# Inverse of the RWKV solve from its transposed twin: 32x32 block transposes on the vector engine in place of a third family of products

## What is computed

```python
def step(state, inp):
    r_t, w_t, k_t, v_t, a_t, b_t = inp
    sa = jnp.einsum("bhvk,bhk->bhv", state, a_t)
    state = (state * w_t[:, :, None, :] + sa[..., None] * b_t[:, :, None, :]
             + v_t[..., None] * k_t[:, :, None, :])
    return state, jnp.einsum("bhvk,bhk->bhv", state, r_t)
...
merged = (jax.nn.sigmoid(z[..., 0:D]) * (ya @ w_merge_a[l])
          + jax.nn.sigmoid(z[..., D:2 * D]) * (yb @ w_merge_b[l])
          + jax.nn.sigmoid(z[..., 2 * D:3 * D]) * (yc @ w_merge_c[l]))
```

## Time and profile before

| | |
|---|---|
| median of 3 runs | 1112.46 us (1112.19, 1112.46, 1114.2) |
| profiled execution, span from first to last instruction | 1114.1 us |
| PE busy | 1096.3 us, 98% |
| DVE busy | 839.7 us, 75% |
| ACT busy | 582.3 us, 52% |
| L2078, products of the solve, both layers | 1792 records, 58.3 us of matmul |

### The profile page before, as it was taken

One profiled execution on the slowest core, in us unless ns is written; L12 is line 12 of the kernel. 1 busy time (PEld: TensorE's weight loads), 2 busy tenths in 40 slices (PEclk: granted clock), 3 DMA queues, 4 the chain that ended last, 5 costly groups with the idle time before them and its releaser, 6 DMA issues.

```text
span 1114.1 us, 24347 instructions
## 1 busy us (share of the span) xinstructions
PE 1096.3 (98%) x10172; PEld 1006.3 (90%) x10172; DVE 839.7 (75%) x1245; ACT 582.3 (52%) x894; POOL 125.6 (11%) x142
## 2 busy tenths in 40 slices
PE   8999999999999999999999999999999999999997
PEld 7889987888789999999989999888887999999997
DVE  4798998665478798987758899957545878888763
ACT  2266577622275666663455575772226556666533
POOL 0100000146002000001110000003530010000001
PEclk8999999999999999999999999999999999999999
DMA  9946555444145566668845546351513465555551
GB/s 379 340 161 224 175 193 210 153 153 154 60 168 227 189 241 230 230 241 288 313 153 190 189 158 231 151 208 59 212 56 151 161 256 189 188 185 183 216 209 38
DMA packets 41464, 214.88 MB, mean 193 GB/s; under 512 B 7936, under 2 KB 8320, under 8 KB 22048
## 3 DMA queue, kind: packets, MB, share of 16 engines
q1 hardware_dynamic: 29856, 171.65, 41.9%
q0 software_dynamic: 11520, 41.95, 10.5%
HBM read 212.01 MB, written 1.05 MB: 191 GB/s over the span
## 4 chain that ended last, share of the span: by engine, by line
PE 95%; DVE 2%; ACT 2%; issue 1%; DMA 0%; DVEq 0%; ACTq 0%
PE ps L1780 17%; PE ps L1778 17%; PE ps L1779 17%; PE ps L1967 6%; PE ps L1969 6%; PE ps L1973 6%; PE ps L1798 5%; PE ps L2078 5%; PE ps L1737 1%; PE ps L2252 1%; PE ps L1755 1%; PE ps L2069 1%; PE ps L2056 1%; PE ps L1994 1%; PE ps L1924 1%
## 5 line engine op out<-in xcount | busy, mean ns | idle before, releaser
L963 ACT ACTIVATE WH<-ring 128x1024 fp32r<-128x1024 f32 x144 | 151.9, 1060 | 164.6 <-PE ps L1780 157.4
L1628 DVE TENSOR_TENSOR WLO<-ring,WH 128x1024 fp32r<-128x1024 f32 x144 | 175.7, 1233 | 70.0 <-ACT WH L963 70.0
L1780 PE MATMUL ps<-HH,WLO 128*128 128x256 f32 x736 | 208.1, 283 | 0.0
L1779 PE MATMUL ps<-HL,WH 128*128 128x256 f32 x736 | 206.6, 281 | 0.0
L1778 PE MATMUL ps<-HH,WH 128*128 128x256 f32 x736 | 205.0, 279 | 0.0
L1780 PEld LDWEIGHTS ps<-HH,WLO 128*128 128x128 f32 x736 | 138.7, 188 | 0.0
L1778 PEld LDWEIGHTS ps<-HH,WH 128*128 128x128 f32 x736 | 138.5, 188 | 0.0
L1779 PEld LDWEIGHTS ps<-HL,WH 128*128 128x128 f32 x736 | 138.0, 188 | 0.0
L561 POOL DMA_DIRECT2D mring<-wmod_dram x80 | 43.2, 540 | 759.4 <-DVE macc L1113 447.6
L1780 PE MATMUL ps<-GH,WLO 128*128 128x256 f32 x384 | 108.3, 282 | 0.0
L1778 PE MATMUL ps<-GH,WH 128*128 128x256 f32 x384 | 108.2, 282 | 0.0
(11 more groups left out here) (403 smaller groups left out, 2592.7 us busy)
## 6 DMA issues: line engine op xcount, KB each, us to landing
ring<-wmain_dram SPq DMA_DIRECT2D x150, 1024.0 KB, 4.9
mring<-wmod_dram POOLq DMA_DIRECT2D x80, 512.0 KB, 5.0
G<-wmod_dram SPq DMA_DIRECT2D x3, 1024.0 KB, 9.7
R<-wmod_dram SPq DMA_DIRECT2D x3, 1024.0 KB, 17.5
TK<-wmod_dram SPq DMA_DIRECT2D x2, 1024.0 KB, 20.7
X<-x_t_dram SPq DMA_DIRECT2D x1, 1024.0 KB, 5.2
y_dram<-H SPq DMA_DIRECT2D x4, 256.0 KB, 2.2
SW<-small_dram SPq DMA_DIRECT2D x1, 512.0 KB, 13.8
```

The costliest lines, as they stand in the source:

```text
L963: A(WH[:, n % 2, part], ring[:, b, part], ACT.Copy).then_inc(hi_ready, 1)
L1628: V.tensor_tensor(WLO[:, n % 2, part], ring[:, b, part], WH[:, n % 2, part].bitcast(F32), ALU.subtract).then_inc(lo_ready, 1)
L1779: MM(out, w_high[:, at], low, start=False, stop=False, skip_group_check=True)
L1780: return MM(out, w_low[:, at], high, start=False, stop=stop, skip_group_check=True)
```

## The change

Step `xt` is gone. After the additions to `TTm` of both parities in a level v < 4, DVE transposes each 32x32 block of `TTm` into `Tm` (`V.transpose`, 128x512, one for a parity). Up to that level T has nothing outside diagonal blocks of 32, so the blocks' transposes are the whole transpose. Step `x` of the next level waits for this on a new semaphore. The fill table has two entries for a level in place of three, and DVE's work between the steps stands at other points.

```diff
-FILL = [8, 32, 48, 32, 36, 8, 20, 8] + [8] + [6, 8, 6] * 4 + [6, 6, 0]
+FILL = [8, 32, 48, 32, 36, 8, 20, 8] + [8] + [8, 8] * 4 + [6, 0]
...
-        for kind in ("m", "x", "xt"):
-            if kind == "xt" and v == len(LEVELS) - 1:
-                continue
+        for kind in ("m", "x"):
...
                         if par == 1 and v == 0:
                             branch_low(1, YBL[:, :, :], YB[:, :, :], YH[:, :, :])
-                        elif par == 1 and v != 2:
-                            dve_chunks((0, 20, 0, 23, 25)[v], (0, 21, 0, 24, 26)[v])
+                        elif par == 1:
+                            mod_beside(1)
                     else:
-                        T_ = (TTm if kind == "x" else Tm)[:, par]
-                        V.tensor_tensor(T_, T_, oct(b), ALU.add).then_inc(t_ev, 1)
-                        if par == 1 and v < 4:
-                            if (kind, v) in (("x", 0), ("xt", 1), ("x", 2), ("xt", 3)):
-                                dve_chunks((19, 21, 22, 24)[v], (20, 22, 23, 25)[v])
+                        V.tensor_tensor(TTm[:, par], TTm[:, par], oct(b), ALU.add).then_inc(t_ev, 1)
+                        if par == 1 and v < len(LEVELS) - 1:
+                            for p2 in range(2):
+                                dve.wait_ge(t_ev, base + step_no("x", p2, v) + 1)
+                                V.transpose(flat(Tm[:, p2]), flat(TTm[:, p2])).then_inc(t_turned, 1)
+                            if v == 3:
+                                gated(2)
                             mod_beside(1)
...
-                    elif kind == "x":
+                    else:
                         pe.wait_ge(t_ev, base + step_no("m", par, v) + 1)
                         if v:
-                            pe.wait_ge(t_ev, base + step_no("xt", par, v - 1) + 1)
+                            pe.wait_ge(t_turned, 8 * l + 2 * (v - 1) + par + 1)
                         block_products(b, Tm[:, par], Mm[:, par], t_mm)
-                    else:
-                        block_products(b, Mm[:, par], Tm[:, par], t_mm)
                     if par == 1:
-                        fill(LEVEL0 + 3 * v + ("m", "x", "xt").index(kind))
+                        fill(LEVEL0 + 2 * v + ("m", "x").index(kind))
```

More of the change, by code:

```diff
@@ L432, in trunk_kernel @@
                                             sem("akv_summed"), sem("akv_ready"))
+        t_turned = sem("solve_turned")
         zy_mm, zy_ev, rb_mm, rb_ev = sem("zy_summed"), sem("zy_ready"), sem("read_products"), sem("read_ready")
```

## The result

| | before | after |
|---|---|---|
| median | 1112.53 us (4 runs, 1112.19 to 1114.2) | 1136.86 us (4 runs, 1127.47 to 1146.91) |
| ratio of after to before | | 1.0181, 95% interval 1.0144 to 1.0218 |
| span of the profiled execution | 1114.1 us | 1134.4 us |
| mean granted clock over it | 0.990 | 0.966 |

The kernel got slower by about 1.8%. The forecast was 1103.4 us, its range ended at 1107.8, and 0.94 of the chance lay on faster. The scatter is new as well: the four executions of after lie 19 us apart, those of before 2 us.

What follows compares the result with a forecast made beforehand. PE, busy for 98% of the span, was taken as the bound. -17.7 (steps) + 1.8 + 5.8 (waits) - 1.4 (`YCL`) + 2.4 (clock) = -9.1 us, from 1112.46 to 1103.4 us; range 1099.8 to 1107.8.

Steps and rivals of the forecast that it cites:

- What goes: PE in the solve: eight `xt` steps of 2.21 us vanish, 17.7 us saved; stream products are only moved.
- What DVE does instead: DVE in the solve: each 128x512 transpose takes 0.65 us, near an addition's 0.69; upper bound 1.34 us.
- The estimate of 1.24 us: DVE transpose priced from the skill page, four 128x128 two-byte tiles at 311 ns; sum worse by 1.5 us.
- rivals that rest on slow transposes: Solve on DVE: transposes of 1.1 to 1.34 us, 1105.5 to 1107.5 us, chance 0.17; about 2.4 us, 1118 us, 0.04.
- Is it hidden?: Solve levels: PE covers DVE's transposes, up to 1.7 us at levels 0 to 2, 0.87 us at level 3.
- I add nothing: Solve levels: the tightest modulation transfer lands half a microsecond late, using only DVE idle time; no cost.
- First new wait: PE at L2120, behind the last `x`: waits 0.9 us for the last addition, 1.8 us over two layers.
- Second new wait: PE before the read part: late `gated(3)` delays the masks, 2.9 us a time, 5.8 us in all.
- What comes back: PE before merge 4: the wait for `YCL` goes, 1.4 us gained over two layers.
- The clock: Behind the read-part wait, both layers: half speed for some 3.3 us, 1.2 us a layer, 2.4 us in all.
- the clock holds: Rival: the clock stays up through the 2.9 us wait before the read part; -11.5 us, 1101.0 us, chance 0.27.
- The slower one: Rival in the solve: transposes of say 2.4 us delay masks and `x` steps; +5.7 us, 1118 us, chance 0.04.

Runs made afterwards that it cites:

- both: Kernel after with six products behind the last `x`, FILL_ZY 10 for 6, and level 4's modulation step moved behind the last additions: 1096.89 us, 0.9853.
- behind: Kernel before, all products kept and no transposes, only the fills of the solve cut by 22 products: 1137.05 us, 1.0256.
- mod_moved: Kernel after with the modulation step behind level 4's masks moved behind the last additions, ahead of `gated(3)`: 1127.84 us, 1.014.
- zy16: Kernel after with FILL_ZY 16 for 6, so merge 3 ends before the read products: 1104.33 us, 0.9925.
- chain8: Kernel after with eight stream products in place of four at each gap of the chain: 1123.29 us, 1.0115.
- spread: Fastest repaired kernel (1096.89 us) with modulation steps in pairs behind the transposes and `gated(2)` behind level 4's masks: 1100.13 us, 0.9891.

## Why the prediction was wrong

- **What goes** was right: 1280 records for 1792, and both's account closes to 2.7 us with 17.7.
- **What DVE does instead** was right: 0.68 us for 0.65, between the bounds. The estimate of 1.24 us was almost twice too long. The rivals that rest on slow transposes are out.
- **Is it hidden?** held at the levels: L2079 waits 1.5 us in all, and transfers that landed late (DVE idle for 1.1 us before 246.56, for 0.16 us before 258.34) used up idle time only. But the count took 1.2 us for every modulation step, and three in each layer took 2.8 to 3.3 us. "I add nothing" should have been 1.5 us.
- **First new wait** failed in its size: "L2120 will wait for 0.9 us" took 2.85. The step "the last addition ends 2.85 us after the `x` starts" took DVE as free then. `behind` and mod_moved, where it is free, gave 0.8. Worth 2 x 1.95 = 3.9 us.
- **Second new wait** was right to a tenth: 2.85 us for 2.9.
- **What comes back** was right: the `YCL` wait is gone.
- **The clock** is the step that failed, in the price and not in the place: "I expect the fall behind the second new wait, in both layers" came true, but priced from the earlier trace rows at "some 3.3 us" of half clock, 1.2 us a layer. It measured 15.9 and 9.3 us. In those rows the fall had 128x512 products of the stream and full 128x128 transposes behind it; here it has the chain, groups of small products with four products of the stream between them, and the clock did not come back for 20 to 37 us. I took the length of a fall as fixed where it depends on what PE does afterwards. A fall behind the first new wait, 1.6 us in layer 0, was not in the sum at all. The runs zy16, behind and chain8 together show this: wait away, no long fall; wait without transposes, the long fall; denser chain, a shorter one.
- **The rivals.** Had the clock held, the account above gives 1107.9 us for the profiled execution, still faster than before: the sign of the result hangs on the clock alone. But the rival "the clock holds" has 1114.1 - 11.5 = 1102.6 us for it. The 5.3 us between are the first wait (3.9) and the masks (1.5), so with the clock held the change gains 6.2 us, and not 11.5. Yet no rival was slower for the clock. The slower one rested on transposes, which rows bounded; the price without an upper bound was the clock's. The chain between the read parts took 20.96 us before, so both chains at half speed, up to 2 x 21 us more, was the end that the range lacked.

## What to carry to other kernels

A wait of PE like the ones here (2.2 and 2.85 us) is priced with the stretch behind it: if that is a chain of short groups, reckon with all of it at half clock, and put the wait where dense work follows, or cover it. Work taken off the critical engine can move another instruction's due time: whatever marked the end of a batch by position (here merge 3) has to be looked up again in the new order. And a vector instruction with both sources in SBUF is costed by what POOL does at that moment.

## What was not expected of the hardware

- The granted clock stayed at 0.50 for up to 37.5 us while PE was busy all the time. Where it came back differs: behind the chain in layer 0 of after, inside it in layer 1 (after 20.5 us), and after 10.2 us in chain8. It is not certain to fall: one kernel's executions ranged from 1106.9 to 1137.8 us.
- A stop of PE without a wait for another engine counts as well. In the solve's preparation one of 1.90, 1.95 and 2.08 us (after, both, spread) had a fall of 3.4 us behind it each time; stops there of up to 0.98 us in six other traces had none.
- A modulation step on DVE started under POOL's 2.4 us subtraction ended 1.1 us after POOL each time (2.77, 3.25, 2.98 us for 1.26); in the twelve traces 60 steps ended 1.08 or 1.09 us behind a subtraction. It goes the other way as well: where the step started 0.59 us ahead (before, 783.12) it kept its 1.28 us, and POOL's subtraction took 2.92 us in place of 2.4. A 128x512 block transpose of four-byte numbers took 0.68 us and was not held.
